# The scan's step sizes computed with the weights stationary and the tokens moving, then brought back to token rows by a selector matmul

## The chip, the cores and the metric

One core of one Trainium2 chip runs the whole kernel. The metric is device microseconds from start to end of one execution; the median of three executions stands for a kernel. All numbers in the program are float32.

## The reference, cut to what matters

The kernel is one inference step of a one-layer trunk for two streams that share the weights: 256 prompt frames and 64 sample frames, 320 tokens in all, model width 2048. The layer normalises, projects with one wide input matrix `w_in` (2048 x 5136), runs two head groups side by side (a chunked gating MLP, and a Mamba-2 scan with 16 heads), projects out, normalises again, and runs a mixture of 16 experts. The last 16 columns of the input projection are the scan's raw step sizes, one per head and token:

```python
proj = h @ w_in[l]                                  # (tokens, 5136)
u, v, z, xbc, dt_raw = jnp.split(proj, SPLITS, axis=-1)   # dt_raw: (tokens, 16)
...
dt = jax.nn.softplus(dt_raw.astype(f32) + dt_bias.astype(f32))
a = -jnp.exp(a_log.astype(f32))
y, h_final = ssd_scan(xs, dt, a, bm, cm, h0.astype(f32))
```

So 320 x 2048 values `h` are multiplied with 2048 x 16 weights. Everything in the scan that depends on time (decays, cumulative sums, scaled inputs) starts from `dt`.

## The kernel before, in words

Each engine has its own program, written out by hand, and the engines meet at counting semaphores only. One SBUF tensor, `arena`, holds everything at fixed offsets; eight PSUM banks PB[0] to PB[7] take the matmul results. SyncE issues the big weight transfers (2 MB each) into slots; a slot is filled again when TensorE has counted its last use up (`slot_used`).

`hT` holds the normalised, modulated activations with the model dimension on the partitions: 16 tiles (KT = 16) of 128 rows by 320 tokens. On TensorE the order around the change is this. A loop over four groups of 512 input columns computes the scan's x, B and C parts (line 896: weights stationary, the 320 tokens of `hT` moving, results in PB[0] to PB[3]); between the halves of a group TensorE does pieces of the conditioning projection `ada` (line 810: the condition vectors, 32 columns wide, stationary in one of four column groups of the array, 512 weight columns moving, result in PB[7]). Then comes a loop `for n in range(4, 10)` (line 1035) over six more groups of 512 columns. Each group is cut into four quarters of four tiles each. A quarter is eight matmuls for the two prompt blocks (`prompt_rows`, line 817: 128 tokens of `hT` stationary, 512 weight columns moving) and eight for the sample block (`sample_rows`, line 823). After the second and the fourth quarter of a group stand two `ada` pieces, and after each quarter the small matmuls of the scan that the table `HOOKS` names (line 257). The same table gives ScalarE and VectorE the order of their own parts.

The step sizes are the first hook, `dt`, after the first quarter of group 4 (lines 908 to 916). For each of the three token blocks (128, 128 and 64 tokens) and each of the 16 tiles, the tokens of `hT` are the stationary operand and the 16 step-size columns `wdt` move. That is 48 matmuls, and the results have tokens on the partitions, three pieces of 16 columns in PB[7]. The hook waits for `modrow_out` 5, that is until ScalarE has moved the conditioning rows out of PB[7] (line 592). Right behind it stands the hook `cs` (lines 917 to 923): 16 transposes of the convolution's last rows into PB[3] to PB[6], waiting for GpSimd's copies (`raw_saved`).

VectorE has first to finish the depthwise convolution of the last four channel tiles (lines 1262 to 1276). Then it clears `dtt`, waits for `dtp` (TensorE's step sizes), adds the bias (line 1284), counts `dt_read` up, and runs a softplus of some 25 small instructions (lines 1287 to 1302), in which ScalarE does one exponential (line 722). At its end `adt_ready` lets TensorE's hook `cum` start (lines 924 to 933, after the second quarter of group 4), which makes the cumulative sums. ScalarE's exponential stands in its program ahead of its copies of the `cs` banks (line 675). TensorE's next `ada` piece also waits for `dt_read`, since it overwrites PB[7].

Of the kernel before, what the change touches and what calls it, by code (L numbers as in the profile page):

```python
# [28 lines left out]
AX = mybir.AxisListType  # L29
# [3 lines left out]
KT = D // P  # L33
SEQ, DEC = 256, 64
TOK = SEQ + DEC
NT = [128, 128, 64]
OFF = [0, 128, 256]
STREAM = [0, 0, 1]
GMW, HEADS, HD, NG, NS = 1024, 16, 64, 4, 128
# [38 lines left out]
def trunk(nc, x_prompt, x_sample, state_ssm, state_conv, c_prompt, c_sample, norm1_g, norm2_g, w_ada, b_ada,  # L78
# [4 lines left out]
    with ctx:  # L83
# [7 lines left out]
        def at(off, *dims):  # L91
            size = 1
            for d in dims:
                size *= d
            assert off + size <= TOTAL
            v = arena[:, off:off + size]
            if len(dims) == 2:
                v = v.rearrange("p (a b) -> p a b", a=dims[0])
            if len(dims) == 3:
                v = v.rearrange("p (a b c) -> p a b c", a=dims[0], b=dims[1])  # L100
            return v

        def take(*dims):
            size = 1
            for d in dims:
                size *= d
            off = ptr[0]
            ptr[0] += size
            return at(off, *dims)
# [5 lines left out]
        ident, upper, after, before, ones, iota = (take(P) for _ in range(6))  # L115
# [3 lines left out]
        wdt = take(KT, HEADS)  # L119
# [14 lines left out]
        edc = take(3, 3, HEADS)  # L134
        st = take(96)
        br = take(2, 20)
        small_end = ptr[0]

        R1 = ptr[0]
# [13 lines left out]
        hT = at(HT, KT, TOK)  # L153
        ZB = HT + 5120
        z = at(ZB, 3, 1024)
        VB = ZB + 3072
# [6 lines left out]
        lng = at(TE, 2, 1024)  # L163
        stT = at(TE + 2048, 2, 1024)
        WT = at(TE + 4096, 8, P)
        END = TE + 5120
        stout = at(SA, 16, P)

# [35 lines left out]
        PB = [ctx.enter_context(nc.psum_tensor(f"bank{i}", [P, N], F32)) for i in range(8)]  # L204
# [11 lines left out]
        cond_in, rows_in, gmraw_in, straw_in, small_in = map(sem, ("cond_in", "rows_in", "gmraw_in", "straw_in", "small_in"))  # L216
        consts, pe_consts, cT_clear, cT_ready = map(sem, ("consts", "pe_consts", "cT_clear", "cT_ready"))
        ssq, var, std, xn = map(sem, ("ssq", "var", "std", "xn"))
        xT, hT_v, hT_s = map(sem, ("xT", "hT_v", "hT_s"))
        rowsT, rows_out, gmT, gm_out_v, stTp, st_out = map(sem, ("rowsT", "rows_out", "gmT", "gm_out_v", "stTp", "st_out"))  # L220
# [3 lines left out]
        dtp, dt_read, adt_ready, cum, cum_out, spe = map(sem, ("dtp", "dt_read", "adt_ready", "cum", "cum_out", "spe"))  # L224
# [29 lines left out]

        HOOKS = {0: ["dt", "cs"], 1: ["cum"],
# [542 lines left out]
        def _(pe):  # L800
            mm, tr = nc.tensor.matmul, nc.tensor.transpose
# [31 lines left out]
            for t in range(KT):  # L833
                for j in range(3):
# [5 lines left out]
                    last = tr(PB[3 + t % 4][:, OFF[j]:OFF[j] + n], x[0:n, j, :].rearrange("q (p t) -> q t p", t=KT)[:, t, :], ident[0:n, 0:n])  # L840
# [10 lines left out]
            for h in range(8):  # L851
                last = tr(PB[1 + h // 4][:, P * (h % 4):P * (h % 4) + P], gmraw[:, h, :], ident)
# [5 lines left out]
            for c in range(8):  # L858
                last = tr(PB[3 + c // 4][:, P * (c % 4):P * (c % 4) + P], straw[:, c, :], ident)
# [24 lines left out]
            with pe.Fori(0, 2) as i:  # L884
                for c in range(2):
# [3 lines left out]
                    for half, slot in ((0, W0), (1, W1)):  # L889
# [4 lines left out]
                        for ch in range(4):  # L894
                            for t in range(8):
                                last = mm(PB[ch][:, 0:TOK], lhsT=slots_w[slot][:, t, ch * P:ch * P + P], rhs=hT[:, 8 * half + t, :],  # L896
                                          start=(half == 0 and t == 0), stop=(half == 1 and t == 7))
# [7 lines left out]
            def hook(name):  # L905
                kind, j = name[:2], int(name[2:3]) if name[2:3].isdigit() else 0
                n, o = NT[j], COFF[j]
                if name == "dt":

                    pe.wait_ge(modrow_out, 5)  # L910
                    pe.wait_ge(small_in, 176)
                    for t in range(3):
                        for k in range(KT):
                            last = mm(PB[7][0:NT[t], 16 * t:16 * t + 16], lhsT=hT[:, k, OFF[t]:OFF[t] + NT[t]], rhs=wdt[:, k, :],  # L914
                                      start=(k == 0), stop=(k == KT - 1))
                    last.then_inc(dtp, 1)
                elif name == "cs":

                    pe.wait_ge(raw_saved, 16)
                    for c in range(16):  # L920
                        last = tr(PB[3 + c // 4][0:6, P * (c % 4):P * (c % 4) + P], cst[:, pos(c), :], ident)
                        if c % 4 == 3:
                            last.then_inc(cs_t, 1)
                elif name == "cum":
# [3 lines left out]
                    for t in range(3):  # L928
# [3 lines left out]
                        last = mm(PB[3][:, 48 * t + 32:48 * t + 48], lhsT=ones[0:r, :], rhs=adt[0:r, t, :], start=True, stop=True)  # L932
                    last.then_inc(cum, 1)
                elif kind == "sa":
# [9 lines left out]
                    for c in range(12):  # L944
                        last = tr(PB[4 + c // 4][0:n, P * (c % 4):P * (c % 4) + P], xin[:, pos(c), o:o + n], ident)
# [4 lines left out]
                elif kind in ("sb", "sc"):  # L950
                    for g in (0, 1) if kind == "sb" else (2, 3):
                        if kind == "sc":

                            k = g - 2
# [73 lines left out]
            def diag(j, g, n):  # L1028
# [3 lines left out]
                              rhs=xdt[0:n, HD * h:HD * h + HD], start=True, stop=True)  # L1032
                last.then_inc(ydiag, 1)

            for n in range(4, 10):
                if n == 4:
                    pe.wait_ge(xin_out, 17)
                elif n < 7:
                    pe.wait_ge(z_out, 4 * (n - 4))
                elif n < 9:  # L1040
                    pe.wait_ge(v_out, 4 * (n - 6))
                else:
                    pe.wait_ge(u_out, 4)
                for quarter in range(4):
                    slot, half = (W0, W1)[quarter // 2], quarter // 2
                    if quarter % 2 == 0:
                        arrived(slot, 5 + n)
                    for t in range(4 * quarter, 4 * quarter + 4):
                        prompt_rows(PB[0:2], hT, t, slots_w[slot][:, t % 8, :], t == 0, t == KT - 1)
                    for t in range(4 * quarter, 4 * quarter + 4):  # L1050
                        last = sample_rows(PB[2], hT, t, slots_w[slot][:, t % 8, :], t == 0, t == KT - 1)
                    if quarter % 2:
                        last.then_inc(slot_used[slot], 1)
                        if n < 8:
                            if n % 2 == 0 and half == 0:
                                pe.wait_ge(modrow_out, n // 2 + 3)
                                pe.wait_ge(dt_read, 1)
                            for a, slot_a in ((0, A0), (1, A1)):
                                arrived(slot_a, 2 * n + 5 + half)
                                ada(slot_a, 8 * (n % 2) + 4 * half + 2 * a)  # L1060
                    for name in HOOKS.get(4 * (n - 4) + quarter, []):
                        hook(name)
# [146 lines left out]
        def _(dve):  # L1209
# [5 lines left out]

            V.memset(cT, 0.0).then_inc(cT_clear, 1)
            V.memset(st, 1.0).then_inc(cT_clear, 1)
            dve.wait_ge(iota_int, 2)
            V.tensor_copy(iota, iota.bitcast(I32))
            V.tensor_copy(tok, tok.bitcast(I32))  # L1220
# [55 lines left out]
                step.end(2)  # L1276


            step(V.memset(dtt, 0.0))
            dve.wait_ge(small_in, 176)  # L1280
            dve.wait_ge(dtp, 1)
            for j in range(3):
                n = NT[j]
                last = V.tensor_tensor(dtt[0:n, j, :], PB[7][0:n, 16 * j:16 * j + 16], hb[0:n, 0, :], ALU.add)
            last.then_inc(dt_read, 1)
            dve.wait_ge(dt_read, 1)
            V.scalar_tensor_tensor(spz, dtt, -1.0, dtt, ALU.mult, ALU.max).then_inc(dt_abs, 1)
            dve.wait_ge(spe, 1)
            step(V.tensor_scalar(spp, spq, 2.0, None, ALU.add))
# [391 lines left out]
```

## Time and profile before

| what | value |
|---|---|
| three executions | 1430.35 us (median), 1426.56, 4198.51 |
| the profiled execution | 1430.36 us, of which the span from first to last instruction is 1428.3 us |
| mean granted TensorE clock over the span | 0.924 |
| busy: TensorE matmul / weight load | 1198.2 us (84%) / 643.5 us (45%) |
| busy: VectorE / ScalarE / GpSimd | 310.4 (22%) / 200.8 (14%) / 116.0 us (8%) |
| moved by DMA | 401.09 MB, mean 281 GB/s |

A float32 matmul shows as two records in the trace, so 48 matmuls are 96 records; a transpose shows as one. Ends of matmuls are modelled, so stretches on TensorE are best read from start to start. The granted clock is a share of full speed: 1.00 is 2.4 GHz, 0.50 is 1.2 GHz.

### The profile page before, as it was taken

How to read it: one execution, taken by the hardware profiler on the slowest of the kernel's cores; microseconds unless marked ns; L12 is line 12 of the kernel's file. 1: busy time of each engine (PE TensorE's matmuls, PEld its weight loads, DVE VectorE, ACT ScalarE, POOL GpSimd, SP SyncE). 2: the span in 40 equal slices, each digit the busy share in tenths (PEclk: the TensorE clock that was granted, in tenths of full speed). 3: DMA queues.
4: the chain of work that ended last, by engine and by line, in shares of the span. 5: the costliest groups of instructions: out<-in, count | busy, mean ns of one | idle time of the engine just before them, and what ended most of it. 6: DMA issues, size and time to landing. Idle time of an engine off the chain costs nothing.

```text
span 1428.3 us, 16027 instructions
## 1 busy us (share of the span) xinstructions
PE 1198.2 (84%) x6320; PEld 643.5 (45%) x6321; DVE 310.4 (22%) x623; ACT 200.8 (14%) x385; POOL 116.0 (8%) x129
## 2 busy tenths in 40 slices
PE   2678999999999999999992299999988788778740
PEld 0225565565545445545542244444544444444420
DVE  0101222131122224120018500111111211111128
ACT  2001111012021222100012100010111111111102
POOL 2010000000000002000005100000000000000016
PEclk8778999989999999999995599999999999999975
DMA  9997787737557529642530468877999999999953
GB/s 333 421 350 279 282 336 291 278 143 294 232 197 281 230 73 357 225 189 77 226 118 33 177 247 305 308 276 296 378 413 412 414 412 402 393 412 412 425 204 105
DMA packets 71717, 401.09 MB, mean 281 GB/s; under 512 B 6489, under 2 KB 6713, under 8 KB 39645
## 3 DMA queue, kind: packets, MB, share of 16 engines
q1 hardware_dynamic: 63216, 368.59, 66.0%
q0 software_dynamic: 6944, 23.99, 5.1%
q10 hardware_dynamic: 1520, 7.98, 1.4%
q8 instruction: 28, 0.46, 0.1%
q14 instruction: 9, 0.07, 0.0%
HBM read 394.85 MB, written 17.22 MB: 288 GB/s over the span
## 4 chain that ended last, share of the span: by engine, by line
PE 65%; DMA 26%; DVE 6%; issue 1%; ACT 1%; SPq 0%; POOLq 0%; DVEq 0%
DMA arena<-in_w_up_dram 20%; PE bank L817 20%; PE bank L896 10%; PE bank L1163 8%; PE bank L823 5%; DMA arena<-in_w_ada_dram 5%; PE bank L810 5%; PE bank L1160 5%; PE bank L1186 4%; PE bank L914 1%; PE bank L1183 1%; DMA arena<-expert_rows 1%; PE bank L840 1%; DVE arena L1480 1%; DVE arena L1481 1%
## 5 line engine op out<-in xcount | busy, mean ns | idle before, releaser
L817 PE MATMUL bank<-arena 128*128 128x512 f32 x640 | 286.0, 597 | 0.0
L1160 PE MATMUL bank<-arena 128*64 128x256 f32 x1536 | 185.8, 399 | 59.9 <-DMA arena<-in_w_gate_dram 32.6
L817 PEld LDWEIGHTS bank<-arena 128*128 128x128 f32 x640 | 117.9, 190 | 135.5 <-issue 134.4
L1160 PEld LDWEIGHTS bank<-arena 128*64 128x64 f32 x1536 | 112.5, 143 | 138.0 <-DMA arena<-in_w_gate_dram 44.8
L896 PE MATMUL bank<-arena 128*128 128x320 f32 x512 | 143.2, 440 | 3.8 <-DVE arena L1258 3.8
L810 PE MATMUL bank<-arena 128*32 128x512 f32 x768 | 101.4, 669 | 44.5 <-DMA arena<-in_w_ada_dram 32.7
L896 PEld LDWEIGHTS bank<-arena 128*128 128x128 f32 x512 | 97.9, 192 | 51.1 <-issue 7.8
L1163 PE MATMUL bank<-arena 128*128 128x512 f32 x256 | 113.5, 604 | 7.5 <-issue 7.5
L1183 PE MATMUL bank<-arena 128*64 128x512 f32 x384 | 85.0, 595 | 6.0 <-DVE arena L1629 6.0
L1626 DVE SCALAR_TENSOR_TENSOR arena<-bank,arena 128x512 f32<-128x512 f32 x16 | 12.0, 751 | 348.5 <-PE bank L1160 232.4
L1163 PEld LDWEIGHTS bank<-arena 128*128 128x128 f32 x256 | 49.5, 194 | 70.2 <-issue 70.2
L823 PE MATMUL bank<-arena 128*64 128x256 f32 x640 | 76.1, 384 | 0.0
L810 PEld LDWEIGHTS bank<-arena 128*32 128x32 f32 x768 | 23.4, 118 | 110.8 <-issue 53.2
L823 PEld LDWEIGHTS bank<-arena 128*64 128x64 f32 x640 | 43.1, 137 | 41.0 <-issue 22.5
L1186 PE MATMUL bank<-arena 128*128 128x512 f32 x128 | 56.0, 595 | 2.0 <-DVE arena L1629 2.0
L1183 PEld LDWEIGHTS bank<-arena 128*64 128x64 f32 x384 | 27.4, 137 | 54.1 <-issue 51.1
L510 POOL DMA_INDIRECT arena<-h_rows,arena x18 | 17.4, 968 | 411.4 <-issue 342.7
L769 ACT ACTIVATE arena<-bank 128x512 f32<-128x512 f32 x34 | 20.3, 598 | 201.5 <-PE bank L1146 201.5
L1636 DVE COPY arena<-bank 128x512 f32<-128x512 f32 x32 | 20.6, 686 | 120.5 <-PE bank L1183 69.7
L1146 PE MATMUL bank<-arena 128*128 128x128 f32 x272 | 34.9, 284 | 8.0 <-DMA arena<-h_rows,arena 8.0
L788 ACT ACTIVATE arena<-bank 128x512 f32<-128x512 f32 x32 | 17.4, 595 | 152.9 <-PE bank L1183 93.3
L1186 PEld LDWEIGHTS bank<-arena 128*128 128x128 f32 x128 | 24.0, 190 | 31.0 <-issue 31.0
(314 smaller groups left out, 856.8 us busy)
## 6 DMA issues: line engine op xcount, KB each, us to landing
arena<-in_w_ada_dram SPq DMA_DIRECT2D x48, 2048.0 KB, 14.9
arena<-in_w_gate_dram SPq DMA_DIRECT2D x32, 2048.0 KB, 26.3
arena<-in_w_up_dram SPq DMA_DIRECT2D x32, 2048.0 KB, 27.1
arena<-in_w_down_dram SPq DMA_DIRECT2D x32, 2048.0 KB, 26.2
arena<-in_w_in_dram SPq DMA_DIRECT2D x20, 2048.0 KB, 7.8
arena<-in_w_out_dram SPq DMA_DIRECT2D x8, 2048.0 KB, 8.8
arena<-mod_final POOLq DMA_DIRECT2D x6, 1024.0 KB, 11.8
arena<-expert_rows SPq DMA_DIRECT2D x8, 512.0 KB, 8.6
```

What stands on the lines that cost most here:

```text
L510: pool.indirect_dma_start(out=Xe[0:n], out_offset=None, in_=h2_d, in_offset=bass.IndirectOffsetOnAxis(ap=iin[0:n].bitcast(U32), axis=0), b ...
L769: act.activation(XeT[:, 4 * k:4 * k + 4, :], PB[2 + k][:, :].rearrange("p (c l) -> p c l", c=4), ACT.Copy).then_inc(XeT_s, 1)
L810: last = mm(PB[7][32 * j:32 * j + 32, :], lhsT=cT[:, t, :], rhs=slots_ada[slot][:, t - t0, j * N:j * N + N], start=(t == 0), stop=(t == KT ...
L817: last = mm(banks[j][:, :], lhsT=xT_[:, t, OFF[j]:OFF[j] + P], rhs=w, start=start, stop=stop)
L823: last = mm(bank[DEC * k:DEC * k + DEC, 0:HALF], lhsT=xT_[:, t, SEQ:TOK], rhs=w[:, HALF * k:HALF * k + HALF], start=start, stop=stop)
L896: last = mm(PB[ch][:, 0:TOK], lhsT=slots_w[slot][:, t, ch * P:ch * P + P], rhs=hT[:, 8 * half + t, :], start=(half == 0 and t == 0), stop= ...
L1146: last = tr(PB[2 + k][:, P * c:P * c + P], Xe[:, P * t:P * t + P], ident)
L1160: last = mm(PB[bank][64 * h:64 * h + 64, 0:HALF], lhsT=XeT[:, t0 + t, 0:64], rhs=slots_w[slot][:, t, HALF * h:HALF * h + HALF], start=star ...
L1163: last = mm(PB[bank][:, :], lhsT=XeT[:, t0 + t, :], rhs=slots_w[slot][:, t, :], start=start, stop=stop)
L1183: last = mm(PB[2 + c // 2][64 * (c % 2):64 * (c % 2) + 64, :], lhsT=hidT[:, q:q + 64], rhs=w, start=(t == 0), stop=(t == 3))
L1186: last = mm(PB[2 + c // 2 + 2 * (c % 2)][:, :], lhsT=hidT[:, P * t:P * t + P], rhs=w, start=(t == 0), stop=(t == 3))
L1636: V.tensor_copy(Ye[:, k * N:k * N + N], PB[2 + k][:, :]).then_inc(Ye_v, 1)
```

## The change

A tile `sel` (128 x 16) is made once, early, on VectorE: row 32g + c has a one in column c, for the four groups g and c under 16; all other rows are zero. Ahead of the loop over groups 4 to 9, TensorE now runs 16 matmuls in which the 16 columns of `wdt` are stationary and all 320 tokens of `hT` move. Tile k goes to the column group k % 4 of the array, so that the partial sums of four tiles each stand at partitions 0, 32, 64 and 96 of PB[4]. VectorE copies that bank (128 x 320) to `dtrow`, after its convolution and ahead of clearing `dtt`. The hook `dt` now stands behind `cs` and is three matmuls: a token block of `dtrow` stationary, `sel` moving, which adds the four partial sums and puts tokens on the partitions again, in PB[7] as before. `cs` waits for the copy, since its transposes write PB[4].

```diff
+        sel = take(HEADS)
...
+        dtrow = at(VB, TOK)
...
-        HOOKS = {0: ["dt", "cs"], 1: ["cum"],
+        HOOKS = {0: ["cs", "dt"], 1: ["cum"],
...
                 if name == "dt":
 
+                    pe.wait_ge(pe_consts, 2)
+                    pe.wait_ge(dt_read, 1)
                     pe.wait_ge(modrow_out, 5)
-                    pe.wait_ge(small_in, 176)
                     for t in range(3):
-                        for k in range(KT):
-                            last = mm(PB[7][0:NT[t], 16 * t:16 * t + 16], lhsT=hT[:, k, OFF[t]:OFF[t] + NT[t]], rhs=wdt[:, k, :],
-                                      start=(k == 0), stop=(k == KT - 1))
+                        last = mm(PB[7][0:NT[t], 16 * t:16 * t + 16], lhsT=dtrow[:, OFF[t]:OFF[t] + NT[t]], rhs=sel, start=True, stop=True)
                     last.then_inc(dtp, 1)
                 elif name == "cs":
 
                     pe.wait_ge(raw_saved, 16)
+                    pe.wait_ge(dt_read, 1)
...
+            pe.wait_ge(small_in, 176)
+            pe.wait_ge(st_out, 2)
+            for k in range(KT):
+                g = 32 * (k % 4)
+                last = mm(PB[4][g:g + 16, 0:TOK], lhsT=wdt[:, k, :], rhs=hT[:, k, :], start=(k < 4), stop=(k >= KT - 4))
+            last.then_inc(dtp, 1)
+
             for n in range(4, 10):
...
-                                pe.wait_ge(dt_read, 1)
+                                pe.wait_ge(dt_read, 2)
...
+            dve.wait_ge(pe_consts, 1)
+            V.tensor_reduce(sel.unsqueeze(2), ident.rearrange("p (g c) -> p c g", g=4)[:, 0:HEADS], AX.X, ALU.add).then_inc(pe_consts, 1)
             dve.wait_ge(iota_int, 2)
...
+            dve.wait_ge(dtp, 1)
+            V.tensor_copy(dtrow, PB[4][:, 0:TOK]).then_inc(dt_read, 1)
             step(V.memset(dtt, 0.0))
             dve.wait_ge(small_in, 176)
-            dve.wait_ge(dtp, 1)
+            dve.wait_ge(dtp, 2)
...
-            dve.wait_ge(dt_read, 1)
+            dve.wait_ge(dt_read, 2)
```

On TensorE, from the end of the loop over the scan's columns to the first `ada` piece of group 4, the order was this (lines of the kernel before: 817 and 823 are a quarter, 914 is `dt`, 921 is `cs`):

```order
L884 COMPARE_AND_BRANCH
L817 MATMUL bank<-arena 128x512 [waits slot0_in,xin_out]
L817 MATMUL bank<-arena 128x512 x7
L823 MATMUL bank<-arena 64x256 x8
L914 MATMUL bank<-arena 128x16 [waits small_in,modrow_out]
L914 MATMUL bank<-arena 128x16 x31
L914 MATMUL bank<-arena 64x16 x16
L921 MATMUL bank<-arena 6x128 [waits raw_saved]
L921 MATMUL bank<-arena 6x128 x15
L817 MATMUL bank<-arena 128x512 x8
L823 MATMUL bank<-arena 64x256 x8
L810 MATMUL bank<-arena 32x512 [waits slot2_in,dt_read,modrow_out]
```

Now it is this (lines of the changed kernel, where 819, 825 and 812 are the old 817, 823 and 810, 1041 is the new matmul with the weights stationary, 923 is `cs`, and 916 is the selector):

```order
L886 COMPARE_AND_BRANCH
L1041 MATMUL bank<-arena 16x320 [waits st_out,small_in]
L1041 MATMUL bank<-arena 16x320 x15
L819 MATMUL bank<-arena 128x512 [waits slot0_in,xin_out]
L819 MATMUL bank<-arena 128x512 x7
L825 MATMUL bank<-arena 64x256 x8
L923 MATMUL bank<-arena 6x128 [waits dt_read,raw_saved]
L923 MATMUL bank<-arena 6x128 x15
L916 MATMUL bank<-arena 128x16 [waits modrow_out,dt_read,pe_consts]
L916 MATMUL bank<-arena 128x16
L916 MATMUL bank<-arena 64x16
L819 MATMUL bank<-arena 128x512 x8
```

The 48 matmuls behind the first quarter became 16 ahead of it and three behind `cs`; `cs` moved in front and has a second wait.

On VectorE, at the end of the convolution's loop, the order before was this (1271 is the convolution, 1284 adds the bias to the step sizes, 1287 begins the softplus):

```order
L1271 SCALAR_TENSOR_TENSOR arena<-arena 128x323
L1262 REGISTER_ALU
L1262 COMPARE_AND_BRANCH
L1279 MEMSET arena 128x48
L1284 TENSOR_TENSOR arena<-bank,arena 128x16 [waits dtp,small_in,dve_step]
L1284 TENSOR_TENSOR arena<-bank,arena 128x16
L1284 TENSOR_TENSOR arena<-bank,arena 64x16
L1287 SCALAR_TENSOR_TENSOR arena<-arena 128x48 [waits dt_read]
```

And it is now this (1291 is the copy of the bank to `dtrow`, 1297 adds the bias, 1300 begins the softplus):

```order
L1282 SCALAR_TENSOR_TENSOR arena<-arena 128x323
L1273 REGISTER_ALU
L1273 COMPARE_AND_BRANCH
L1291 COPY arena<-bank 128x320 [waits dtp]
L1292 MEMSET arena 128x48
L1297 TENSOR_TENSOR arena<-bank,arena 128x16 [waits dtp,small_in,dve_step]
L1297 TENSOR_TENSOR arena<-bank,arena 128x16
L1297 TENSOR_TENSOR arena<-bank,arena 64x16
L1300 SCALAR_TENSOR_TENSOR arena<-arena 128x48 [waits dt_read]
```

One copy came in between the convolution and the clearing of `dtt`; the bias and the softplus follow as before.

## Rows read from the trace of the kernel before

**Rows 1.** The page's chain that ended last, shares of the span by line.

```profile
DMA arena<-in_w_up_dram 20%; PE bank L817 20%; PE bank L896 10%; PE bank L1163 8%; PE bank L823 5%; DMA arena<-in_w_ada_dram 5%; PE bank L810 5%; PE bank L1160 5%; PE bank L1186 4%; PE bank L914 1%; PE bank L1183 1%; DMA arena<-expert_rows 1%; PE bank L840 1%; DVE arena L1480 1%; DVE arena L1481 1%
```

**Rows 2.** The chain around the change: start us, us, what.

```profile
262.83 17.48 PE bank L896 x64
280.30 3.57 PE bank L810 x32
283.87 7.06 PE bank L817 x16
...
292.81 14.43 PE bank L914 x96
307.24 3.00 PE bank L921 x16
310.24 6.87 PE bank L817 x16
...
322.56 0.33 PE bank L930 x2
322.88 0.22 PE bank L931 x2
...
324.22 0.12 PE bank L931 x2
...
333.60 1.46 PE bank L945 x12
```

**Rows 3.** TensorE by stretch: us, PE busy (records), PEclk, DMA share, GB/s.

```profile
292.75:297.50 4.75, 4.75 (x38) 0.84 0.95 395
297.50:302.00 4.50, 4.50 (x23) 0.50 0.02 8
307.20:310.10 2.90, 2.90 (x18) 0.59 0.00 0
...
322.50:324.60 2.10, 2.10 (x23) 1.00 1.05 409
...
333.50:335.80 2.30, 2.30 (x23) 1.00 1.03 424
```

**Rows 4.** The chain at a later line 945, behind a wait of TensorE.

```profile
410.32 1.92 ACT arena L707 x7
...
412.38 2.79 PE bank L945 x12
```

**Rows 5.** Line 840, the first transposes of the kernel, in stretches as above.

```profile
64.00:74.00 10.00, 10.00 (x34) 0.50 1.02 424
```

**Rows 6.** VectorE's timeline: start us, us, instruction, idle before it and releaser.

```profile
291.57 0.10 DVE L1279 MEMSET arena<- 128x48 f32 x1
307.38 0.33 DVE L1284 TENSOR_TENSOR arena<-bank,arena 128x16 f32<-128x16 f32 x3 [15.71 <-PE bank L914]
...
313.43 0.21 DVE L1302 SCALAR_TENSOR_TENSOR arena<-arena 128x48 f32<-128x48 f32 x1
```

**Rows 7.** Groups, shapes apart: busy us, mean ns of one, then idle before and releasers.

```profile
L810 PEld LDWEIGHTS bank<-arena 128*32 128x32 f32 x768 | 23.4, 118 | 110.8 <-issue 53.2 <-DMA arena<-in_w_ada_dram 46.0 <-ACT arena L577 11.5
...
L1230 DVE COPY arena<-bank 128x320 f32<-128x320 f32 x8 | 3.9, 491 | 31.2 <-PE bank L840 31.2
```

**Rows 8.** ScalarE's timeline: last copy of the scan's columns, then the conditioning rows.

```profile
281.83 0.30 ACT L630 ACTIVATE arena<-bank 128x64 f32 x1
...
292.12 0.58 ACT L592 ACTIVATE arena<-bank 128x512 f32 x1
```

**Rows 9.** VectorE's timeline in the start of the kernel.

```profile
33.17 0.17 DVE L1222 TENSOR_SCALAR arena<-arena 128x3 f32<-128x3 f32 x1 [29.93 <-ACT arena L585]
```

**Rows 10.** All engines by stretch: us, busy of PE, PEld, DVE, ACT, POOL, PEclk, DMA share, GB/s.

```profile
700.00:800.00 100.00, 64.52 (x285) 36.47 (x283) 46.79 (x80) 13.30 (x22) 22.64 (x5) 0.78 0.26 95
...
1000.00:1200.00 200.00, 167.87 (x1220) 95.75 (x1220) 33.00 (x86) 27.93 (x40) 12.65 (x13) 0.97 1.00 405
```

**Rows 11.** The whole chain in order of time, the first expert: start us, us, what.

```profile
822.77 30.54 PE bank L1163 x64
```

## The prediction

> **What bounds the kernel now.** I read the chain that ended last first. TensorE's lines carry most of it, the experts' weight transfers are next, and the step sizes, line 914, stand in it with 1% [rows 1]. The chain around the change, piece by piece, has no gap: the loop over the scan's columns, the conditioning pieces, the first quarter of group 4, then 14.43 us of line 914, then 3.00 us of `cs`, then the next quarter [rows 2]. TensorE is the bound here, and each microsecond that it does not spend moves all that comes after. The third view is the same place by stretches, with the clock. Line 914 starts at full clock and falls to 0.50, and `cs` still runs at mostly 0.50 [rows 3]. The DMA share in the second stretch of line 914 is 0.02: the weight transfers have caught up with TensorE and wait for it. So 14.43 us is not the price of 48 matmuls at full clock; it is the price of 96 records that move 16 columns each, for most of which the clock is halved. In the stretch at 0.84 there are 38 records in 4.75 us, in the one at 0.50 there are 23 in 4.50 us. Last I read VectorE and ScalarE beside it, to see who waits: VectorE is done at 291.67 us and sits idle for 15.71 us until line 914 ends [rows 6].
>
> **The change part by part.** The sum is made against the profiled execution's own time, 1430.36 us (a span of 1428.3 and 2.06 around it), which is also the median of the three.
>
> *Removed:* line 914, 14.43 us on the path [rows 2].
>
> *Added, the 16 matmuls with weights stationary.* The nearest row is line 810: 16 matmuls, stationary 32 columns in one of four column groups, 512 columns moving, in 3.57 us [rows 2]. The new ones have 16 columns in the same four groups, and 320 columns moving: 3.57 x 320/512 = 2.23 us. The other end is line 896, 320 columns moving with the full array, 64 records in 17.48 us or 0.273 us each; if the groups did not run side by side, 32 records would take 8.74 us. I take 2.23, because the groups and the order of the tiles are those of line 810, and keep 8.74 for the range. I see no reason for less than 2.23.
>
> A rule speaks against the lower price. In the trace, line 896 moves 320 columns in 0.273 us, 0.853 ns for each column; 512 columns would then take 0.437 us and the eight rounds of line 810 (four records side by side in each) 3.50 us, of the 3.57 that they take [rows 2]. So 0.07 us are left for weight loads, though the mean load of line 810 is 0.118 us long [rows 7]. The Trainium skill, "TensorE: Matmul & The Clock Gate", Part 3 ("Packing small matmuls"), has it that a weight load overlaps running matmuls only where the row group differs, and here all four column groups use all rows. By that rule each of the eight rounds would show one load, 8 x 0.118 = 0.94 us more, and the sum would be 1418.2 us; the row says that they are hidden, and I go by the row.
>
> *Added, the selector:* three matmuls with 16 columns moving. The hook `cum` has the same shapes at full clock, 0.22 us for a matmul with 128 stationary columns and 0.12 us for a small one [rows 2], so 0.22 + 0.22 + 0.12 = 0.56 us. At half clock it would be double, 1.1 us.
>
> *Changed in price, `cs`:* 16 transposes take 3.00 us behind line 914, at 0.59 of the clock [rows 2, 3]. The 12 transposes of line 945 take 1.46 us in a stretch with clock 1.00, and 2.79 us where they follow a wait of TensorE [rows 2 to 4]. By that ratio `cs` at full clock takes 3.00 x 1.46/2.79 = 1.57 us, a gain of 1.43 us. Whether the clock stays up is the question. In the new order it is 1.57 us of transposes and 0.56 us of small matmuls, 2.1 us between two dense quarters. The trace has two such stretches: `cum`, 2.1 us, and the transposes at 333.5 us, 2.3 us, both at 1.00 [rows 3]. So I take the full clock; 3.00 us is the other end.
>
> *The new waits.* TensorE's `cs` waits for VectorE's copy. What is queued behind it on TensorE is all the rest, so each microsecond of lateness counts whole. TensorE gets there at 283.87 + 2.23 + (292.81 - 283.87) = 295.0 us. The copy starts when VectorE is done with the convolution: the clearing that followed it began at 291.57 [rows 6], and the partial sums are there since 286.1. The nearest copy from a bank to SBUF of the same shape takes 0.49 us [rows 7], so it lands at 292.1 us, 2.9 us ahead. The selector also waits for the conditioning rows to leave PB[7], done at 292.70 [rows 8], and TensorE gets there at 296.6. The 16 new matmuls wait for small loads on which ScalarE has already waited (line 619) ahead of its copies of the scan's columns, and for nothing else; those copies are through at 282.1 [rows 8], so the quarter after them does not wait either. What is behind: the softplus. From the end of line 914, 307.24, to the end of its last instruction, 313.64, are 6.4 us [rows 2, 6]; now it starts at 295.0 + 1.57 + 0.56 = 297.1 and ends at 303.5. TensorE asks for it at `cum`, after the quarter and the `ada` pieces, 322.56 - 310.24 = 12.32 us after 297.1, at 309.5: 6 us of cover, where there were 8.9. ScalarE's copies of the `cs` banks stand behind its exponential, so they come after the selector now, some 2 us after `cs`; `cum` needs them at 309.5 too, and they are hidden.
>
> *At nothing:* the making of `sel` lies in the first microseconds of VectorE, which then idles until 33.17 us [rows 9]. The copy to `dtrow` lies in the 15.71 us that VectorE waited.
>
> *What is late next.* Nothing on the weight side: transfers stood still at 0.02 before TensorE went on, so slots are full. The stage until the router stays bound by TensorE.
>
> *Sum:* 14.43 + 1.43 - 2.23 - 0.56 = 13.07 us less, 1430.36 - 13.07 = **1417.3 us**.
>
> **The rivals.** *The groups run one after another.* Against it stands line 810; for it, that no row has 16 stationary columns spread over the four groups. Time: 1430.36 - 14.43 - 1.43 + 8.74 + 0.56 = 1423.8 us. That is also the case in which the change doesn't do what it says.
>
> *The clock falls all the same.* For it: line 840, 10 us of transposes at 0.50 [rows 5], and line 945 behind a wait [rows 4]. Against it: the two stretches of 2.1 and 2.3 us at 1.00 [rows 3]. Price: `cs` stays at 3.00 (1.43 more), the selector doubles (0.56), and the dense quarter behind it, 8.94 us at full clock as above, loses up to some 2 us before the clock is back: about 4, so 1421.3 us.
>
> *The gain is given back in the experts.* There the chain is weight transfers, 20% of the span [rows 1], and from 1000 us the DMA share is 1.00 [rows 10]: if the end were set by a stream of bytes that starts at a fixed time, the time would stay at 1430.4 us. Against it: between 700 and 800 us the DMA share is 0.26 [rows 10], and the chain returns to TensorE's line 1163 at 822.77 [rows 11]. The stream waits for slots that TensorE frees, so it moves with TensorE.
>
> *Slower: the copy comes too late.* `cs` stands still until VectorE's convolution and the copy are through. It costs from 295.0 us on, one for one, and eats the whole gain when the copy lands after 295.0 + 13.1 = 308.1 us, 16 us later than I work out; then TensorE's idle time would bring the half clock too, as at line 945 (2.79 for 1.46), and the time would be about 1432 us. For it: only that the copy is new on a path from TensorE to VectorE and back. Against it: VectorE's end at 291.57 does not hang on line 914 at all [rows 6].
>
> **How the numbers follow.** My case 0.77, groups in a row 0.07, clock 0.08, given back 0.05, too late 0.03. The range: the fastest of the three runs, 1426.56, less 13.07 is 1413.5; stretches of half clock elsewhere may fall otherwise when all moves by 13 us, and the longest matmul piece that I priced, line 945, shows 1.33 us for one, so three of them make 1410 us. Above, 1423.8 and some 2 us of the runs' own spread: 1426 us. It holds the first three cases but for their tails. About 2%, 28.6 us, is what a measurement of this kernel can tell from no change; no case comes near it on either side, since all of line 914 and `cs` together is 17.4 us. I leave 0.01 for faster and 0.02 for slower (one of three runs took far longer for no reason in the kernel), and 0.97 between.
>
> **What would show it.** Right: the 16 new matmuls from about 284 to 286 us; no fall of the clock at 297; `cs` in about 1.6 us from about 295; TensorE at the second quarter at 297 instead of 310; VectorE's idle time ahead of the bias some 5 us instead of 15.7; the router and the experts shifted by 13 us and otherwise alike. Wrong: the new matmuls in more than 4 us; TensorE idle ahead of `cs` with VectorE as releaser; a PEclk of 0.50 in 295 to 300; or a shift that is 13 us at 400 us and gone at 1400.

## The result, and the profile after

| | before | after |
|---|---|---|
| median of the executions timed together | 1428.45 us | 1412.61 us (1408.37 to 1415.83) |
| profiled execution / span | 1430.36 / 1428.3 us | 1412.09 / 1410.0 us |
| ratio after to before | | 0.987, 95% interval 0.9841 to 0.9899 |

The ratio, which leaves out the one execution of 4198.51 us, says 1.3% faster, or 18.6 us of 1428.45, with an interval of 14.4 to 22.7 us; the two medians in the table are 15.8 us apart. The forecast time, 1417.3 us, stood for 13.07 us less. The direction is right and the time lies in the range, but the interval of 14.4 to 22.7 us lies above the forecast gain. The later comparisons of the same two kernels, with 17 to 23 executions of before, give 19.2 us (after_again) and 15.4 us (after_b); the interval of the last, 12.6 to 19.4 us, holds 13.07. So the excess is some 2 to 6 us, and the traces have to say where it is.

The chain around the change, in the trace after. It answers to [rows 2]; lines 819 and 825 are the old 817 and 823, 812 the old 810, 1041 the new matmuls, 923 `cs`, 916 the selector, 932 `cum`.

```profile
277.84 3.57 PE bank L812 x32
281.41 2.16 PE bank L1041 x32
283.56 7.06 PE bank L819 x16
290.63 1.88 PE bank L825 x16
292.50 1.84 PE bank L923 x16
294.35 0.57 PE bank L916 x6
294.92 7.06 PE bank L819 x16
301.98 1.88 PE bank L825 x16
303.86 3.57 PE bank L812 x32
307.43 0.33 PE bank L932 x2
```

From the end of the `ada` pieces to `cum` it is 307.43 - 281.41 = 26.02 us now. Before it was 322.56 - 283.87 = 38.69 us [rows 2]. The site of the change gained 12.67 us in this pair of traces, against 13.07 worked out.

TensorE there by stretches (stretch, us, PE busy and records, PEclk, DMA share, GB/s), which answers to [rows 3]. The clock does not fall any more:

```profile
281.41:283.57 2.16, 2.16 (x33) 1.00 1.05 406
...
292.50:294.35 1.85, 1.85 (x20) 1.00 1.01 422
294.35:294.92 0.57, 0.57 (x7) 1.00 0.80 331
```

VectorE's timeline after, which answers to [rows 6]: the copy ends at 289.54 us, 3.0 us before `cs` begins, and the wait ahead of the bias went from 15.71 to 5.45 us.

```profile
289.06 0.48 DVE L1291 COPY arena<-bank 128x320 f32<-128x320 f32 x1
289.50 0.10 DVE L1292 MEMSET arena<- 128x48 f32 x1
295.05 0.33 DVE L1297 TENSOR_TENSOR arena<-bank,arena 128x16 f32<-128x16 f32 x3 [5.45 <-PE bank L916]
```

So the rest of the gain is not here. Both traces compared instruction by instruction on TensorE give the places: after is ahead by 2.5 us before it comes to the site, by 15.1 behind it, by 13.6 at the router (most of the loss is one late group of transposes, line 945 of before, which met a half clock in after and not in before, 2.74 us for 1.47), and by 18.2 us at the second layer of the first expert. It stays there to the end, 1428.3 - 1410.0 = 18.3. The jump from 13.6 to 18.2 stands at TensorE's entry into the experts. The chain before, at that place ("issue" is time in which the engine waits for nothing that the profile shows; line 1186 is the second layer):

```profile
816.14 6.63 issue
...
856.56 13.99 PE bank L1186 x32
```

and after:

```profile
802.57 0.55 issue
803.12 2.85 PE bank L1172 x6
805.96 2.53 issue
808.49 26.62 PE bank L1172 x58
...
838.36 13.99 PE bank L1195 x32
```

Before, TensorE stood for 6.63 us and then ran line 1163, the first expert, in one piece [rows 11]. In the trace this time is one instruction, the branch of line 1202 that chooses between an expert with few rows and one with many, 6.44 us long; after, it is 0.37 us long, and a stall of 2.53 us comes six records later. Nothing in the change touches that branch. But 29 matmuls fewer are 116 instructions fewer in TensorE's program (a weight load and a matmul for each of two records; waits are not counted), so everything behind them stands at another place of the code. The page shows what loads code, the DMA queue of kind "instruction" (packets, MB, share of 16 engines). Before:

```profile
q8 instruction: 28, 0.46, 0.1%
```

and after:

```profile
q8 instruction: 27, 0.44, 0.1%
```

28 packets of 0.46 MB are 16 KB each. The kernels below are built on the reading that such a piece is 256 instructions; after_pad64 tests it.

The trace also has the time of each packet of this queue, and one stands inside each of the two waits. This is the queue's line for the stretch from 816.2 to 822.7 us of before:

```profile
q8 instruction: 1, 0.02, 0.9%
```

The packet runs from 820.19 to 821.10 us, and the expert's first matmul starts at 822.77. After the change it runs from 806.18 to 807.06 us, and the matmuls go on at 808.49. So both kernels wait for the same fetch, which starts 4.0 and 3.6 us after the branch; they differ in whether the expert's first instructions were already there.

### The profile page after: what moved, and what is told of

Its sections match the earlier page's. It is cut to its first block, busy times and chain, and to the rows that moved or that the text cites. A ratio compares the mean times of both kernels' runs of the same rounds, so it can differ in the third digit from the quotient of the medians.

```text
span 1410.0 us, 15915 instructions
## 1 busy us (share of the span) xinstructions
PE 1184.8 (84%) x6262; PEld 629.4 (45%) x6263; DVE 311.0 (22%) x625; ACT 200.6 (14%) x385; POOL 115.4 (8%) x129
## 4 chain that ended last, share of the span: by engine, by line
PE 65%; DMA 27%; DVE 5%; issue 1%; ACT 1%; SPq 0%; POOLq 0%; DVEq 0%
PE bank L819 20%; DMA arena<-in_w_up_dram 20%; PE bank L898 10%; PE bank L1172 8%; PE bank L825 5%; PE bank L812 5%; PE bank L1169 5%; PE bank L1195 4%; DMA arena<-in_w_ada_dram 4%; DMA arena<-in_w_in_dram 2%; PE bank L1192 1%; DMA arena<-expert_rows 1%; DVE arena L1493 1%; DVE arena L1494 1%; PE bank L842 1%
## 5 line engine op out<-in xcount | busy, mean ns | idle before, releaser
L819 PEld LDWEIGHTS bank<-arena 128*128 128x128 f32 x640 | 118.3, 191 | 135.6 <-issue 134.5
L898 PEld LDWEIGHTS bank<-arena 128*128 128x128 f32 x512 | 97.4, 192 | 51.0 <-issue 7.2
L1172 PEld LDWEIGHTS bank<-arena 128*128 128x128 f32 x256 | 49.0, 192 | 66.2 <-issue 66.2
L1155 PEld LDWEIGHTS bank<-arena 128*128 128x128 f32 x272 | 31.3, 146 | 14.8 <-DMA arena<-h_rows,arena 8.1
```

The lines of the kernel that those rows point to most:

```text
L819: last = mm(banks[j][:, :], lhsT=xT_[:, t, OFF[j]:OFF[j] + P], rhs=w, start=start, stop=stop)
L1155: last = tr(PB[2 + k][:, P * c:P * c + P], Xe[:, P * t:P * t + P], ident)
L1172: last = mm(PB[bank][:, :], lhsT=XeT[:, t0 + t, :], rhs=slots_w[slot][:, t, :], start=start, stop=stop)
```

## The experiments

**Is the entry chance or a matter of place?** First both kernels once more, unchanged.

> The kernel before once more, for a second trace. Between the two traces the site of the change gained 12.7 us, and 4.6 us more came at TensorE's entry into the first expert: its branch took 6.44 us in before and 0.37 us (with a stall of 2.53 us a little later) in after. Theory P (place of the code): the wait is for instructions to be loaded and hangs on where the branch's target lies in TensorE's program, so this trace shows a branch of 6.0 to 6.8 us again and a first expert that starts 6.5 to 7.5 us after the last small matmul. Theory C (chance): the entry differs from run to run of one kernel, so it shows anything from 0.4 to 6.5 us. The 2.5 us that after was ahead before the site: both theories let it move by 2 us or so from run to run.

> The changed kernel once more. Theory P: the branch again takes 0.3 to 0.5 us and the stall comes after six records of the first expert; ratio to before 0.985 to 0.990 (14 to 21 us less, 12.7 from the site, 4.6 from the entry, and what the start does by chance). Theory C: the entry may cost 6.5 us here, and the ratio is 0.991 on the mean.

Measured: before_again 1428.07 us, ratio 0.9991 (0.9974 to 1.0008); after_again 1410.67 us, ratio 0.9864 (0.9841 to 0.9887). The second trace of before, around line 914 and at the entry:

```profile
283.55 7.06 PE bank L817 x16
...
292.49 12.49 PE bank L914 x96
...
320.61 0.33 PE bank L930 x2
...
814.46 6.20 issue
820.66 30.78 PE bank L1163 x64
```

The entry repeats: 6.20 us of standing still, the branch 6.02 us long. Line 914 does not: 12.49 us for 14.43, because the clock fell later. TensorE by stretches in that trace:

```profile
292.49:298.00 5.51, 5.51 (x50) 0.97 0.84 348
298.00:304.90 6.90, 6.90 (x49) 0.50 0.01 4
```

From the end of the `ada` pieces to `cum` it is 320.61 - 283.55 = 37.06 us there, so with this trace the site gained 11.0 us instead of 12.67 (37.06 - 26.02). In the second trace of after the branch took 0.36 us again. The stall after six records is not to be seen there, and the half clock of the router stage lasted 5.4 us into the expert:

```profile
804.52 30.60 PE bank L1172 x64
```

The packet with the next piece ran from 807.50 to 808.45 us there, and the seventh record started at 809.94, right behind the sixth: the six slow records had lasted until the code came. The scan's first matmul (line 896 of before) began at 112.56 and 113.46 us in the traces of before, and at 110.80 and 113.89 in those of after: two traces of one kernel differ there by up to 3.1 us, so the 2.5 us ahead of the site need no cause in the change.

Then the place itself was moved, in both directions, by small matmuls that nothing reads, at the very start of TensorE's program, where it waits for data (29 here, and 35, 56 or 64 in the kernels named after them):

```diff
+            pe.wait_ge(pe_consts, 1)
+            for k in range(29):
+                mm(PB[0][0:16, 0:2], lhsT=ident[:, 0:16], rhs=ident[:, 0:2], start=True, stop=True)
             pe.wait_ge(cT_ready, 2)
```

> The changed kernel with 29 small matmuls (116 instructions) added at the very start of TensorE's program, where it waits for data until 11.8 us; their result is not used. They put the expert's branch back to the place in the program that it has in before. Theory P: the branch takes about 6.4 us again, and the kernel is 4 to 5 us slower than the changed one, ratio to before about 0.991. Theory C: no change, ratio as after_again within 0.002.

Measured: 1416.92 us, ratio 0.9914 (0.9893 to 0.9935), 6.2 us slower than after_again beside it, whose interval does not overlap with this one. Its chain at the entry:

```profile
802.72 6.68 issue
809.40 30.51 PE bank L1175 x64
```

With the code where it was before, the long branch is back: from the start of this "issue" row to the second layer it takes 40.4 us, as in before, and 34.4 in after_again, so 6.0 of the 6.2 us are at the entry. The change alone is then worth 1429.88 - 1416.92 = 12.96 us.

> The kernel before with 35 small matmuls (140 instructions) added at the start in the same way. If TensorE's instructions are loaded in pieces of 16 KB, which is 256 instructions of 64 bytes, then 140 more puts the branch where it is in after (116 fewer). Theory P: the branch takes about 0.4 us with a stall of 2.5 us after six records, and the kernel is 4 to 5 us faster than before without any change to the step sizes, ratio about 0.997. Theory C: ratio 1.000.

Measured: 1421.75 us, ratio 0.9954 (0.9934 to 0.9973), 8.1 us less than the 1429.88 of before by the medians and 6.6 us by the ratio, with an interval of 3.9 to 9.4 us. Its chain:

```profile
812.73 0.55 issue
813.28 3.27 PE bank L1166 x7
816.55 2.53 issue
819.08 24.75 PE bank L1166 x57
```

The old kernel with 35 idle matmuls more is faster than without them. The 4 to 5 us expected lie in the interval. The stall comes after seven records and not after six; the count of 140 for 116 leaves out the waits, which the change altered too. In its trace the expert starts 6.1 us sooner after the router's first matmul than in before (21.9 for 28.0), and the first expert takes 33.8 us as before, the stall standing where before had the half clock. At this place of the code the change itself is worth 1421.75 - 1410.67 = 11.1 us (after_again). A control that adds exactly one piece of 256 instructions:

> A control: 64 small matmuls are 256 instructions, one whole piece of 16 KB, so every branch stands where it stands in the changed kernel, modulo one piece. Theory P: as after_b within 1.5 us, with the branch at 0.37 us and the first expert at 33.9 to 35.2 us. Rival (it is the number of instructions at the start, or the early small matmuls, not the place in a piece): the branch or the time moves as in after_pad29, by 6 us.

Measured: 1412.40 us against 1412.51 for the changed kernel beside it (after_b), ratios 0.9883 (0.9857 to 0.9909) and 0.9888 (0.9864 to 0.9912). The chain stands as in after, a short branch and a stall after six records:

```profile
804.59 0.55 issue
805.14 2.84 PE bank L1175 x6
807.98 2.84 issue
810.82 28.17 PE bank L1175 x58
```

So neither the number of added instructions nor the early matmuls matter, only the place in a piece of 256 instructions. Theory C falls and theory P stands. (The first expert with its transposes took 37.1 us there, 2 us more than expected: the granted clock fell to 0.50 during the stall, at 810.1 us, and stayed there for 6.8 us, in after for 3.4.)

**A version without any stall.** If the piece that holds the branch's target holds more of the expert, the next one arrives in time.

> The changed kernel with 56 small matmuls (224 instructions, the same as 32 fewer modulo 256) at the start of TensorE's program. Theory P: after the branch 56 instructions of the expert are already there instead of 24, that is 28 records of 0.43 us, 12 us, which covers the 6 us from the branch to the arrival of the next piece. So neither the branch nor the matmuls stall, the first expert starts 0.5 us after the branch and runs through at full clock, and the kernel is 2.5 to 4 us faster than the changed one, ratio to before about 0.985. Theory C: as after_again.

> The changed kernel with 56 small matmuls at the start, a second time. In its first trace the first expert ran 31.0 us without a stall, 2.9 to 4.2 us less than in the two traces of the changed kernel, but the median was the same within the interval. Theory P: the 2.9 us are real and the start, which came 0.3 to 3.4 us later in that trace, is chance, so it is 2 to 4 us faster than after_b. Rival: the added matmuls cost at the start what the entry saves, so both are alike within 1 us.

> The changed kernel, beside the two padded ones on one chip. Branch into the first expert 0.37 us as in both traces so far; the first expert takes 33.9 to 35.2 us until its second layer. Ratio to before about 0.9865.

Measured: after_b's branch took 0.37 us, and its first expert 34.6 us, both as expected. after_pad56 took the first time 1410.29 us, ratio 0.9869 (0.9847 to 0.9890), no better than the changed kernel on another chip; the second time, on the chip of after_b, 1409.44 us (1405.54 to 1410.36), ratio 0.9862 (0.9838 to 0.9887), where after_b had 1412.51 us (1410.33 to 1414.19). That is 3.1 us in the medians, with intervals that overlap; five of its six executions lie below all six of after_b. The trace shows what it is meant to show, a whole first expert without a stall, in both; this is the second:

```profile
805.05 0.55 issue
805.60 27.76 PE bank L1175 x64
...
836.61 14.00 PE bank L1198 x32
```

The first expert takes 31.0 us from its first matmul to its second layer, against 35.2 in after and 33.8 in before. That the whole kernel gains from it by 3 us is likely, not shown.

All thirteen traces agree on the entry. From the start of the "issue" row to the second layer it takes 40.2 to 40.4 us in the five with the branch at its old place, 34.4 to 37.7 in the six at the place of after, and 31.6 in the two of after_pad56. In the eleven of the first two groups the packet of 16 KB starts 3.5 to 4.2 us after the branch does, and the next matmul starts 1.3 to 1.7 us after the packet's end.

**Are the column groups side by side?**

```diff
-                g = 32 * (k % 4)
-                last = mm(PB[4][g:g + 16, 0:TOK], lhsT=wdt[:, k, :], rhs=hT[:, k, :], start=(k < 4), stop=(k >= KT - 4))
+                last = mm(PB[4][0:16, 0:TOK], lhsT=wdt[:, k, :], rhs=hT[:, k, :], start=(k == 0), stop=(k == KT - 1))
...
-                        last = mm(PB[7][0:NT[t], 16 * t:16 * t + 16], lhsT=dtrow[:, OFF[t]:OFF[t] + NT[t]], rhs=sel, start=True, stop=True)
+                        last = mm(PB[7][0:NT[t], 16 * t:16 * t + 16], lhsT=dtrow[:, OFF[t]:OFF[t] + NT[t]], rhs=ident[:, 0:HEADS], start=True, stop=True)
```

> The changed kernel with all 16 matmuls in one column group (partitions 0 to 15 of the bank, one accumulation), the selector being a piece of the identity. The column groups alone are tested. If they run side by side, as line 810 says, the 32 records take 8.7 us instead of 2.16, and TensorE comes to cs 6.6 us later: ratio to the changed kernel 1.0046. If the gain did not come from the groups, the 16 matmuls take about 2.2 us here too.

Measured: 1419.51 us, ratio 0.9930 (0.9907 to 0.9952), where the changed kernel had 0.9864 and 0.9888 on other chips. In its chain the same 16 matmuls take four times as long:

```profile
284.10 8.62 PE bank L1040 x32
292.72 7.06 PE bank L819 x16
```

The groups are worth 6.5 us of the gain, and they run side by side with 16 columns as with 32. A record takes 8.62/32 = 0.269 us here, and a round of four 2.16/8 = 0.270 us in after, both no longer than the 0.273 us of line 896 for 320 columns: the weight loads are hidden in one group too.

**How much of line 914 was the clock?** The same 48 matmuls in pieces between dense ones; the hook `dt` keeps the first block. In before_split2 the first block, too, goes into the second quarter, after t == 4, and the second after t == 5.

```diff
                     for t in range(4 * quarter, 4 * quarter + 4):
                         prompt_rows(PB[0:2], hT, t, slots_w[slot][:, t % 8, :], t == 0, t == KT - 1)
+                        if n == 4 and t == 4:
+                            step_sizes(1)
+                        if n == 4 and t == 6:
+                            step_sizes(2).then_inc(dtp, 1)
```

> The kernel before with the same 48 matmuls for the step sizes in three pieces: the first token block after the first quarter as before, the second and third between the prompt matmuls of the second quarter. Nothing else changes. Theory K (clock): what fell on line 914 is to a large part the half clock. In pieces of 16 matmuls between dense ones the clock stays at 1.00, a record takes 0.11 us instead of 0.20, the 48 matmuls take 9.0 us instead of 14.4 and cs 1.84 instead of 3.00, so this kernel is about 6.5 us faster than before, ratio 0.9955, which is half of the gain at the site. Rival W (work): the 14.4 us are the price of the shapes whatever the clock, and this kernel is as fast as before, ratio 1.000, or slower if the softplus gets late for cum.

Measured: 1425.30 us, ratio 0.9975 (0.9961 to 0.9989), 3.6 us less and not 6.5. Its chain (line 907 is the step sizes, 923 `cs`):

```profile
291.25 4.82 PE bank L907 x32
296.07 3.41 PE bank L923 x16
...
301.71 3.48 PE bank L907 x32
...
308.72 1.97 PE bank L907 x32
```

In that trace the site took 35.74 us, against 38.69 and 37.06 in the two of before. TensorE by stretches:

```profile
291.20:294.00 2.80, 2.80 (x26) 0.92 1.01 421
294.00:297.00 3.00, 3.00 (x16) 0.50 0.59 246
...
301.70:305.10 3.40, 3.40 (x34) 1.00 0.02 5
308.70:310.60 1.90, 1.90 (x33) 1.00 0.00 0
```

At full clock a block of 128 tokens takes 3.48 us and the one of 64 takes 1.97, so all 48 matmuls take 3.48 + 3.48 + 1.97 = 8.93 us. By that the clock cost 3.6 us of 12.49 or 5.5 of 14.43. A record takes 0.109 us with 128 stationary columns and 0.062 us with 64, though 16 columns move in both, so its price goes with the stationary side, the weight load. The first block and `cs` behind it still met the fall, so this order saves only part of it.

> The kernel before with the 48 matmuls in three pieces, all three between prompt matmuls of the second quarter, and cs alone behind the first quarter. In before_split the clock still fell in the first piece with cs behind it, and the other two pieces ran at full clock in 3.48 and 1.97 us. Theory K: now nothing small is longer than 3.5 us, the clock stays at 1.00, the 48 matmuls take 3.48 + 3.48 + 1.97 = 8.93 us and cs 1.84, against 12.49 to 14.43 and 3.0 to 3.3 in before: 5 to 6.6 us faster than before, ratio 0.9955 to 0.9965. Rival W: the clock falls all the same in the second quarter, and the ratio is 0.998 to 1.000.

Measured: 1425.24 us, ratio 0.9989 (0.9962 to 1.0016), with executions from 1420.86 to 1439.76 us. Inconclusive: the profile shows one of three long executions (1435.29, 1438.32 and 1439.76 us, the other nine took 1427.35 us at most), in which the clock fell among the pieces and dense matmuls between them ran at or near 0.50:

```profile
302.25:305.30 3.05, 3.05 (x6) 0.58 0.00 0
...
309.35:312.90 3.55, 3.55 (x5) 0.50 0.00 0
```

The three have a mean granted clock of 0.917 to 0.922, the nine 0.925 to 0.938. Why one kernel loses the clock in some executions and less in others stays open.

## Why the prediction was wrong, and what of it held

- *Removed, line 914.* 14.43 us in the trace used, 12.49 in another of the same kernel and 12.52 in before_pad35; the difference is when the clock fell and for how long. The term has a spread of 2 us that one trace does not show, and the sum took its dear end.
- *The 16 matmuls, 2.23 us.* Measured 2.16. The dear end, 8.74, is what one group costs: 8.62. The weight loads are hidden, as the row on line 810 said. The rule that the prediction cites from the Trainium skill, "TensorE: Matmul & The Clock Gate", Part 3 ("Packing small matmuls"), that a weight load overlaps only where the row group differs, does not hold here, nor in after_onegroup (0.269 us for a record); the same part also lets a load go ahead when it targets the background weight buffer, which would agree with both.
- *The selector, 0.56 us.* Measured 0.57.
- *`cs`, 1.57 us.* Measured 1.84. The ratio of two line-945 pieces was the wrong way to it; the full-clock piece alone, 1.46 us for 12 transposes, gives 1.95 for 16. With the measured terms the site's sum is 14.43 + 1.16 - 2.16 - 0.57 = 12.86, against 12.67 in the chain. The wait of TensorE did not by itself make line 945 dear: behind the same wait it took 1.47 us at 485.45 us of the trace of before.
- *The clock stays up; the copy comes 2.9 us early; the softplus is covered.* All three as said: 1.00 in the stretches, 3.0 us, and no idle time of TensorE ahead of `cum`. The 2 us that the rival of the falling clock put on the dense quarter have no row: the quarter behind the half clock took 318.99 - 310.24 = 8.75 us in before, no more than the 8.94 at full clock.
- *"The router and the experts shifted by 13 us and otherwise alike."* This step failed. The sum had a term for each instruction that TensorE runs at the site, and none for where the rest of its program comes to stand. The entry of the first expert was a row of the chain of before, 6.63 us of "issue", and it was not asked what that was. The place of the branch in the code is worth 6.2 us (after_pad29 against after_again), or 8.1 us by the medians in the old kernel (before_pad35 against before); it came with the change by luck, and 29 idle matmuls at the start take it away. The whole of 1429.88 - 1410.67 = 19.2 us (after_again) so parts into 13.0 + 6.2 us, or 8.1 + 11.1 us in the other order. That each adds up is no proof, since the same medians stand in both; the traces are, with 11.0 to 12.7 us at the site and 6.0 at the entry.
- *The range.* Its lower end, 1410 us, was taken from stretches of half clock elsewhere, so that 1412.61 us lies in it is partly luck. And the prediction's "about 2%" as what can be told from no change is too wide: the intervals here reach 0.1 to 0.3% to each side.
- *"Nothing on the weight side" is late next, and the gain is not given back in the experts.* Right: 18.2 us at the first expert, 18.3 at the end.

The Trainium skill, "Runtime: NRT & Kernel Launch", section "Instruction fetch mechanics", has the mechanism: code is fetched ahead in order, in blocks of 16 KB, and a taken branch whose target is outside what is loaded has to wait for the fetch. The runs agree: 16 KB packets inside the waits, 6.2 to 6.8 us of "issue" in the five traces where the target was not there, 0.55 to 0.62 us in the eight where it was, and no change with a shift of 256 instructions. By how many blocks the fetch runs ahead, no run here tells.

What the gain is made of, at the site: with all at full clock, the old form costs 8.93 + 1.84 us and the new one 2.16 + 0.57 + 1.84, which is 6.2 us; the clock adds 4.8 to 6.5 us, and makes the 11.0 to 12.7 us of the traces.

## What to carry to other kernels

A row of long "issue" time behind a branch can be code being loaded, as the 6.2 to 6.8 us were here, and then a change that adds or removes instructions ahead of it can move it: price that, or test it by a few idle instructions at the start, before a few microseconds are put down to the change. The 48 small matmuls, whose price goes with their weight loads, cost twice here, once in themselves and once by the half clock into which they fell; turning the operands around and using the four column groups removed both. For a price under another clock, take the row at that clock, not a ratio of two rows of another operation.

## What the runs showed of the hardware that was not expected

The branch into code that is not loaded took 6.0 to 6.6 us on TensorE in all five traces that have it (before, before_again, after_pad29, before_split, before_split2), and moving it by idle instructions changed the whole time by 6 to 8 us. A code load that stalled the matmuls for 2.5 us at full clock (after) was not to be seen at half clock, where the matmuls took longer to use up what was there (after_again). The granted clock at one and the same place of one kernel fell at 295.9 us in one execution and at 297.7 in another, and the site took 1.6 us less in the second.
